# Opening of a two-layer trunk kernel: separate signals for constants, parameters and tokens, and the two parts of the first modulation computed in another order

## The chip, the core and the metric

The program runs on one core of a Trainium2 chip. The metric is the device time of one execution in microseconds (us). A core has TensorE (PE in the profile, its weight loads PEld), VectorE (DVE), ScalarE (ACT), GpSimd (POOL) and SyncE (SP), which here issues nearly all DMA transfers. They run side by side and wait for each other through semaphores. A DMA adds 16 to its semaphore when it has landed.

## What is computed

The reference runs two layers of a trunk. What stands at its very start is the part that matters here:

```python
mod = jax.nn.silu(c) @ w_mod[i] + b_mod[i]
mod_c = jax.nn.silu(c_ctx) @ w_mod[i] + b_mod[i]
sh1, sc1, g1, sh2, sc2, g2 = jnp.split(mod[:, None, :], 6, axis=-1)
h = _modulate(_rmsnorm(x, norm1_g[i]), sh1, sc1)       # h * (1 + scale) + shift
hc = _modulate(_rmsnorm(xc, norm1_g[i]), sh1c, sc1c)
y, yc = _mixer(h, hc, ...)                             # begins with h @ w_in
```

with `_rmsnorm(x, g) = x * rsqrt(mean(x * x) + EPS) * g`. There are 256 latent and 256 context tokens of 1024 channels. After the mixer (a state-space branch and a retention branch) each layer has a product-key expert stage, which takes most of the time.

## The kernel before

Tokens lie transposed in `xT`: 128 partitions, 8 channel blocks (`KD`), 512 tokens. Weights come in units of 128 x 2048 floats (1 MB) into `ring`, which has four slots. SP loads unit u into slot u mod 4 once `used[slot]` says that the unit four places earlier has been read. The modulation matrix of a layer is 24 such units, four (`MOD_W`) for each of the six parts: units 0 to 3 give the shift `sh1`, units 4 to 7 the scale `sc1`.

The work is ordered by hand: every engine has its own block, which walks the same list of stages. The opening is the stage `mod`, then `norm1`, then `front`.

- **SP** (L634 to L646): constants `cst`, parameters `par`, tokens `xT` (2 MB), all on the one semaphore `const_in`, then w_mod units 0 to 7 through the ring, then the first unit of `w_front` and the later units, in the order in which their slots come round.
- **PE**: waits for all three (`const_in` at 48). `norm_mean` multiplies the squares of the tokens with a matrix of 1/1024 (8 matmuls of 512 columns, which the trace shows as 16). `mod_row_of` makes one 256-wide piece of a modulation row from one unit, reading the condition `cond0`, and frees the slot. `mod_columns` turns the finished row `mrow0` into columns, one small matmul for each block of 128 channels. Then come the front products of `norm1`'s result with w_front unit 0: the high part of the weights times the high part of the tokens (`wX`, `hiP`), the low part of the weights (`elo`), then the low part of the tokens (`loP`), then two more modulation units.
- **ACT**: silu of the condition, `cond0`, the squares `hT` (L1480), the state-space parameters (L1554 to L1561), the square root of the mean (`stddev`, L1486, into `rs1`), copies of each row piece from PSUM (L1535), the high part of w_front unit 0 (`front_high`, L1514), and then `shifted` (L1498): token plus shift, into `hiP`.
- **DVE**: the state-space parameters, the reciprocal of `rs1` (`inverted`, L1986), `mod_tables` (L2005 to L2012: bias added, and the gain from the scale), `normed` (L1997: `xT` times gain times `rs1`, 16 halves of 256 tokens), the low part of w_front unit 0 (`front_low`, L2020), and `loP` (L2086), which reads both `xT` and `hiP`.

## Time and profile before

| | us |
|---|---|
| median of 3 runs | 2993.99 |
| lowest and highest | 2991.23, 2996.83 |
| span of the profiled execution | 2986.2 |

| engine | busy us | share of the span |
|---|---|---|
| PE | 2762.6 | 93% |
| DVE | 2404.3 | 81% |
| ACT | 1409.5 | 47% |
| POOL | 405.5 | 14% |

The shares are means over the whole program, so they say little of its first 60 us, in which all that the change touches happens. For that stretch one reads the chain of work that ended last and the timeline. The span runs from the first to the last instruction; the device time has some 8 us more around it.

### The profile page before, as it was taken

Reading aid. Unit: us, or ns where it says so; the run is one execution under the profiler, and the core shown is the slowest. Engines: PE = TensorE matmul, PEld = TensorE weight load, DVE = VectorE, ACT = ScalarE, POOL = GpSimd, SP = SyncE. Lnnn points to the kernel's source line nnn. Section 1 sums busy time; section 2 is a strip of 40 time slices with the busy share of each in tenths; the row PEclk is TensorE's granted clock in tenths of the full one; section 3 lists DMA queues with packets and bytes.
Section 4 is the critical chain, followed back from the end, with each engine's and each line's share of the span. In section 5 each row is a group of like instructions: output and inputs, shape, how many; then the busy total and the mean of one; then the engine's idle time right before and its main releaser. Section 6 shows DMA issues by size and latency. Waiting matters only on the chain.

```text
span 2986.2 us, 52044 instructions
## 1 busy us (share of the span) xinstructions
PE 2762.6 (93%) x18077; PEld 2395.3 (80%) x18077; DVE 2404.3 (81%) x4652; ACT 1409.5 (47%) x2264; POOL 405.5 (14%) x408
## 2 busy tenths in 40 slices
PE   6999999777899999999999998989966999999998
PEld 5878877547788888888888886877855888888887
DVE  5487555998987888878888887787589888898887
ACT  5343432227744444444444444324426666666664
POOL 0000000005422211212212210000005101010110
PEclk9999999879999999999999999999987999999999
DMA  6522222644489898998888883323430688888885
GB/s 247 210 91 86 99 99 107 246 158 159 155 308 320 306 333 297 330 324 305 290 301 291 292 299 129 116 97 103 161 136 29 230 321 310 320 312 318 314 322 209
DMA packets 168663, 677.80 MB, mean 227 GB/s; under 512 B 16464, under 2 KB 50416, under 8 KB 125296
## 3 DMA queue, kind: packets, MB, share of 16 engines
q1 hardware_dynamic: 134816, 432.09, 40.3%
q0 software_dynamic: 33744, 244.37, 22.8%
q8 instruction: 61, 1.00, 0.1%
q14 instruction: 42, 0.34, 0.0%
HBM read 658.63 MB, written 17.69 MB: 226 GB/s over the span
## 4 chain that ended last, share of the span: by engine, by line
PE 80%; DVE 12%; DMA 3%; ACT 2%; issue 1%; SPq 0%; POOL 0%; ACTq 0%; DVEq 0%
PE ps L889 80%; DVE hot L2537 2%; DMA ring<-in_w_mod 1%; DVE hot L2532 1%; DVE hot L2535 1%; DVE loP L2086 1%; DMA gate_scratch<-spill 1%; DVE gst L2238 0%; DMA xT<-x_scratch 0%; DVE rs L1986 0%; DMA xT<-in_x_t 0%; PE ps L1026 0%; DMA mcst<-in_mixer_consts 0%; DVE elo L2032 0%; DVE hx L2249 0%
## 5 line engine op out<-in xcount | busy, mean ns | idle before, releaser
L889 PE MATMUL ps<-h2a,ehi 128*128 128x352 f32 x2048 | 492.6, 323 | 1.4 <-DVE elo L2547 1.4
L815 POOL DMA_INDIRECT gbuf<-in_expert_rows,gidx x192 | 236.1, 1230 | 1438.6 <-DVE yg L2592 1328.3
L1946 ACT ACTIVATE ehi<-ring 128x1024 fp32r<-128x1024 f32 x256 | 271.3, 1060 | 288.5 <-PE ps L889 288.1
L889 PEld LDWEIGHTS ps<-h2a,ehi 128*128 128x128 f32 x2048 | 359.9, 188 | 16.5 <-DVE elo L2547 1.9
L2604 DVE TENSOR_TENSOR elo<-ring,ehi 128x1024 fp32r<-128x1024 f32 x256 | 313.0, 1223 | 69.2 <-ACT ehi L1946 67.2
L889 PE MATMUL ps<-h2b,ehi 128*128 128x192 f32 x2048 | 348.2, 273 | 1.8 <-DVE elo L2547 1.8
L889 PEld LDWEIGHTS ps<-h2b,ehi 128*128 128x128 f32 x2048 | 321.3, 192 | 13.3 <-DVE elo L2547 2.1
L889 PE MATMUL ps<-h2a,elo 128*128 128x352 f32 x1024 | 328.7, 321 | 0.0
L2547 DVE TENSOR_TENSOR elo<-ring,ehi 128x1024 fp32r<-128x1024 f32 x256 | 311.9, 1219 | 14.0 <-ACT ehi L1911 14.0
L889 PE MATMUL ps<-h2b,elo 128*128 128x192 f32 x1024 | 281.8, 275 | 0.0
L1911 ACT ACTIVATE ehi<-ring 128x1024 fp32r<-128x1024 f32 x256 | 268.9, 1051 | 12.0 <-DMA ring<-in_experts 11.9
L2592 DVE SCALAR_TENSOR_TENSOR yg<-gbuf,gw,yg 128x1024 f32<-128x1024 f32 x192 | 245.8, 1280 | 25.9 <-ACT gw L1933 25.9
L889 PE MATMUL ps<-ehi,whA 128*128 128x512 f32 (+1 forms) x768 | 241.5, 395 | 2.3 <-DVE wlA L2628 2.3
L889 PE MATMUL ps<-ehi,wB 128*128 128x512 f32 x768 | 241.1, 395 | 0.0
L889 PE MATMUL ps<-ehi,wlA 128*128 128x512 f32 (+1 forms) x768 | 240.9, 394 | 0.0
L889 PE MATMUL ps<-elo,whA 128*128 128x512 f32 (+1 forms) x768 | 239.8, 393 | 0.0
L2582 DVE SCALAR_TENSOR_TENSOR gbuf<-gbuf,h2n 128x1024 f32<-128x1024 f32 x192 | 234.0, 1219 | 0.1
L889 PEld LDWEIGHTS ps<-h2b,elo 128*128 128x128 f32 x1024 | 197.2, 193 | 0.0
L889 PEld LDWEIGHTS ps<-h2a,elo 128*128 128x128 f32 x1024 | 192.5, 188 | 0.0
L889 PE MATMUL ps<-hot 128*128 128x128 f32 x1088 | 148.5, 291 | 38.4 <-ACT hot L1898 32.1
L889 PEld LDWEIGHTS ps<-hot 128*128 128x128 f32 x1088 | 136.5, 199 | 50.8 <-issue 39.6
L889 PEld LDWEIGHTS ps<-elo,whA 128*128 128x128 f32 (+1 forms) x768 | 137.7, 179 | 41.1
(444 smaller groups left out, 5368.5 us busy)
## 6 DMA issues: line engine op xcount, KB each, us to landing
ring<-in_experts SPq DMA_DIRECT2D x512, 512.0 KB, 6.1
ring<-in_w_mod SPq DMA_DIRECT2D x48, 1024.0 KB, 5.9
ring<-in_w_side SPq DMA_DIRECT2D x24, 1024.0 KB, 5.0
ring<-in_w_front SPq DMA_DIRECT2D x12, 1024.0 KB, 6.4
ring<-in_w_merge SPq DMA_DIRECT2D x16, 768.0 KB, 4.3
ring<-in_w_q SPq DMA_DIRECT2D x12, 1024.0 KB, 7.4
gate_scratch<-spill SPq DMA_DIRECT2D x44, 256.0 KB, 2.0
gateA<-gate_scratch SPq DMA_DIRECT2D x4, 2816.0 KB, 18.2
```

Source lines behind the costliest of these rows:

```text
L815: pool.indirect_dma_start(gbuf[:, k % 2, :], None, a[f"expert_rows{l}"], bass.IndirectOffsetOnAxis(gidx[:, at:at + 1], 0)).then_inc(gather ...
L889: return pe.matmul(out, w, x, start=start, stop=stop, **k)
L1911: act.activation(ehi[:, k % 2, :], ring[:, (u + k) % RING, 0:DM], ACT.Copy).then_inc(uhi_ready, 1)
L1946: act.activation(ehi[:, 2 + k % 2, :], ring[:, (u + k) % RING, DM:2 * DM], ACT.Copy).then_inc(vhi_ready, 1)
L2086: last = v.scalar_tensor_tensor(by_four(loP[:, k, :], s_), by_four_of(scaled(l, k, s_)), modT[:, l, 0, k, side:side + 1], by_four(hiP[:, k ...
L2532: v.tensor_tensor(hot[:, g, 1, 0:2, :], row.unsqueeze(1).to_broadcast([P, 2, P]), idxT[:, 1, 4 * n:4 * n + 2].unsqueeze(2).to_broadcast([P ...
L2535: v.tensor_scalar(hot[:, g, 1, 2, :], row, idxT[:, 1, k:k + 1], idxT[:, 2, k:k + 1], ALU.is_equal, ALU.mult)
L2537: v.tensor_tensor(hot[:, g, 0, :, :], row.unsqueeze(1).to_broadcast([P, 4, P]), idxT[:, 0, 4 * n:4 * n + 4].unsqueeze(2).to_broadcast([P, ...
L2547: v.tensor_tensor(elo[:, r, 0:DM], ring[:, r, 0:DM], ehi[:, k % 2, :].bitcast(F32), ALU.subtract).then_inc(ulo_ready, 1)
L2582: v.scalar_tensor_tensor(rows, rows, 1.0, h2n[:, :], ALU.mult, ALU.mult, accum_out=ga[:, at]).then_inc(dot_ready, 1)
L2592: v.scalar_tensor_tensor(yg[:, :], gbuf[:, n % 2, DM:2 * DM], gw[:, at], yg[:, :], ALU.mult, ALU.add).then_inc(acc_done, 1)
L2604: v.tensor_tensor(elo[:, r, DM:2 * DM], ring[:, r, DM:2 * DM], ehi[:, 2 + b, :].bitcast(F32), ALU.subtract).then_inc(vlo_ready, 1)
```

## The change

Constants, parameters and tokens get semaphores of their own (`par_in`, `cst_in`, and `x_in[0]`, `x_in[1]` for the two halves of the channels). SP loads the parameters, the constants, the four units of the scale, the two halves of the tokens and then the four units of the shift. PE makes the scale's rows and columns, then the mean, then the shift's rows and columns (in PSUM bank 5). ACT moves the squares behind the state-space work and the scale's copies; it waits for the shift's table ahead of `shifted`. DVE makes the scale's table ahead of the reciprocal, and the shift's table inside `normed`, after three of the eight blocks. Two two-turn loops (on PE and ACT) and one on SP are written out.

```diff
-            sp.dma_start(cst[:, :], a["consts"]).then_inc(const_in, 16)
-            sp.dma_start(par[:, :], a["params"]).then_inc(const_in, 16)
-            sp.dma_start(xT[:, :, :], a["x_t"]).then_inc(const_in, 16)
+            sp.dma_start(par[:, :], a["params"]).then_inc(par_in, 16)
+            sp.dma_start(cst[:, :], a["consts"]).then_inc(cst_in, 16)
...
-                    stream(u, a["w_mod"][0, 0:EARLY], EARLY)
+                    for k in range(MOD_W):
+                        load(u + k, a["w_mod"][0, MOD_W + k])
+                    for n in range(2):
+                        part = slice(n * KD // 2, (n + 1) * KD // 2)
+                        sp.dma_start(xT[:, part, :], a["x_t"][:, part, :]).then_inc(x_in[n], 16)
+                    for k in range(MOD_W):
+                        load(u + MOD_W + k, a["w_mod"][0, k])
...
-            pe.wait_ge(const_in, 48)
+            pe.wait_ge(cst_in, 16)
...
+                    def part_columns(s, rows, bank):
+
+                        count(pe, mod_row, rows)
+                        for c in range(s * KD, (s + 1) * KD):
+                            last = mm(ps[:, bank, 2 * c:2 * c + 2], mrow0[:, c * P:c * P + P], cst[:, C_SEL:C_SEL + 2], True, True)
+                        last.then_inc(mod_col, 1)
+
+                    pe.wait_ge(cond_ready, 1)
+                    for k in range(MOD_W):
+                        mod_row_of(u + k, k, k, cond0)
+                    part_columns(1, MOD_W, 4)
                     norm_mean(("norm1", 0, 0), hT, TL)
-                    pe.wait_ge(cond_ready, 1)
-                    mod_rows(u, 0, 0, EARLY, 0, cond0)
-                    mod_columns(0, 0, 2, mrow0, 4)
+                    for k in range(MOD_W):
+                        mod_row_of(u + MOD_W + k, MOD_W + k, k, cond0)
+                    part_columns(0, 2 * MOD_W, 5)
...
-            act.wait_ge(const_in, 48)
+            act.wait_ge(cst_in, 16)
+            act.wait_ge(par_in, 16)
...
+                    elif k % (KD // 2) == 0:
+                        act.wait_ge(x_in[k // (KD // 2)], 16)
...
+                if st == ("norm1", 0, 0):
+                    act.wait_ge(mod_done, 2)
...
-                    squares(("norm1", 0, 0), hT, 0, TL)
...
+                    rows_of(1, 0)
+                    squares(("norm1", 0, 0), hT, 0, TL)
                     stddev(("norm1", 0, 0), rs1, TL)
-                    mod_rows(u, mrow0, 0, EARLY, 0)
+                    rows_of(0, MOD_W)
...
-            dve.wait_ge(const_in, 48)
+            dve.wait_ge(cst_in, 16)
+            dve.wait_ge(par_in, 16)
...
-                if st != ("norm1", 0, 0):
-                    inverted(st, rs, w)
+                inverted(st, rs, w)
                 for k in range(KD):
+                    if st == ("norm1", 0, 0) and k == 3:
+                        mod_tables(0, 0, 1, ps[:, 5, 0:2 * KD], 2)
...
-                    inverted(("norm1", 0, 0), rs1, TL)
-                    mod_tables(0, 0, 2, ps[:, 4, 0:4 * KD], 1)
+                    mod_tables(0, 1, 2, ps[:, 4, 2 * KD:4 * KD], 1)
```

`rows_of(part, first)` is ACT's copy of four row pieces. The rest of the diff counts `mod_col` and `mod_done` one higher in the later stages, since there is one more table.

On PE, from the start of the program, before. `ring,cond` is a modulation unit (8 matmuls), `cst,mrow` the columns, `hT,cst` the mean, and the last three rows are the products of w_front unit 0:

```order
1 L889 MATMUL ps<-hT,cst 128x512 x8
...
5 L889 MATMUL ps<-ring,cond 32x256 x8
6 L585 REGISTER_ALU
7 L889 MATMUL ps<-ring,cond 32x256 x8
8 L585 REGISTER_ALU
9 L889 MATMUL ps<-ring,cond 32x256 x8
10 L585 REGISTER_ALU
11 L889 MATMUL ps<-ring,cond 32x256 x8
12 L913 REGISTER_ALU
13 L913 COMPARE_AND_BRANCH
14 L889 MATMUL ps<-cst,mrow 128x2 x16
15 L889 MATMUL ps<-wX,hiP 128x256 x32
```

And now, in the same place:

```order
1 L895 MATMUL ps<-ring,cond 32x256 x32
2 L895 MATMUL ps<-cst,mrow 128x2 x8
3 L895 MATMUL ps<-hT,cst 128x512 x8
4 L895 MATMUL ps<-ring,cond 32x256 x32
5 L895 MATMUL ps<-cst,mrow 128x2 x8
6 L895 MATMUL ps<-wX,hiP 128x256 x32
7 L895 MATMUL ps<-elo,hiP 128x256 x32
8 L895 MATMUL ps<-wX,loP 128x256 x32
```

The mean has moved from the first place to behind four units and half of the columns, and the other four units stand behind it (before, rows 5 to 11 were a loop of two turns).

On ACT, from the start of the parameters' work, before:

```order
3 L1528 ACTIVATE cond<-par 128x8x2
4 L1480 ACTIVATE hT<-xT 128x512 x8
5 L1554 ACT_TABLE_LOAD
6 L1554 ACTIVATE lg<-par 128x16
7 L1555 ACTIVATE lg<-lg 128x16
8 L1557 ACTIVATE s5w<-par 128x64
9 L1559 ACTIVATE s5w<-s5p 128x64
10 L1560 ACT_TABLE_LOAD
11 L1560 ACTIVATE s5w<-s5w 128x64
12 L1561 ACTIVATE s5w<-s5w,cst 128x64
13 L1486 ACT_TABLE_LOAD
14 L1486 ACTIVATE rs<-ps,cst 128x512
```

And now, from the last of the state-space work:

```order
11 L1582 ACTIVATE s5w<-s5w,cst 128x64
12 L1589 ACTIVATE mrow<-ps 128x256 x4
13 L1500 ACTIVATE hT<-xT 128x512 x8
14 L1506 ACT_TABLE_LOAD
15 L1506 ACTIVATE rs<-ps,cst 128x512
16 L1589 ACTIVATE mrow<-ps 128x256 x4
17 L1536 ACTIVATE wX<-ring 128x2048
18 L1520 ACTIVATE hiP<-xT,modT 128x64x4 x16
```

The squares stand behind the scale's four copies, and the conversion of w_front's first unit stands, as before, behind the last copies and ahead of `hiP`.

On DVE, now, from the last of the state-space work to `loP`:

```order
31 L2108 TENSOR_TENSOR s5p<-s5w 128x64
32 L2037 TENSOR_TENSOR modT<-ps,par 128x16
33 L2043 TENSOR_SCALAR gain<-modT 128x16
34 L2044 TENSOR_TENSOR gain<-gain,par 128x16
35 L2017 RECIPROCAL rs<-rs 128x512
36 L2029 SCALAR_TENSOR_TENSOR xT<-xT,gain,rs 128x256 x6
37 L2037 TENSOR_TENSOR modT<-ps,par 128x16
38 L2029 SCALAR_TENSOR_TENSOR xT<-xT,gain,rs 128x256 x10
39 L2052 TENSOR_TENSOR elo<-ring,wX 128x2048
40 L2117 SCALAR_TENSOR_TENSOR loP<-xT,modT,hiP 128x64x4 x16
```

Before, the reciprocal stood ahead of one table for both parts, and the 16 halves of `xT` in one row behind it.

## Rows read from the trace of the kernel before

**Rows 1.** Chain that ended last, 0 to 110 us: start us, us, what.

```profile
1.65 9.99 DMA xT<-in_x_t
...
13.39 12.81 PE ps L889 x80
...
26.21 9.80 DMA ring<-in_w_mod
...
36.13 1.11 PE ps L889 x16
...
37.79 3.75 PE ps L889 x32
...
42.28 6.43 DVE xT L1997 x16
48.70 2.20 DVE elo L2020
50.91 9.58 DVE loP L2086 x16
60.49 0.04 issue
60.53 49.64 PE ps L889 x449
```

**Rows 2.** Timeline: start us, us, engine, line, operation, count [idle before <-releaser].

```profile
11.66 0.21 ACT L1551 ACTIVATE par<-par 128x16 f32<-128x16 f32 x1 [9.63 <-DMA xT<-in_x_t]
12.63 4.25 ACT L1480 ACTIVATE hT<-xT 128x512 f32<-128x512 f32 x8
13.39 9.17 PE L889 MATMUL ps<-hT,cst 128*128 128x512 f32 x16 [13.39 <-ACT hT L1480]
```

**Rows 3.** DMA totals of 0 to 12 us, then of 20 to 40 us.

```profile
DMA packets 574, 3.74 MB, mean 312 GB/s; under 512 B 60, under 2 KB 188, under 8 KB 316
...
ring<-in_w_mod SPq DMA_DIRECT2D x6, 1024.0 KB, 4.9
ring<-in_w_front SPq DMA_DIRECT2D x2, 1024.0 KB, 8.7
```

**Rows 4.** Timeline: modulation units on PE, ACT's copy, the columns.

```profile
28.68 1.07 PE L889 MATMUL ps<-ring,cond 128*32 128x256 f32 x16 [2.53 <-DMA ring<-in_w_mod]
31.16 1.93 PE L889 MATMUL ps<-ring,cond 128*32 128x256 f32 x16 [1.41 <-DMA ring<-in_w_mod]
37.36 0.38 ACT L1535 ACTIVATE mrow<-ps 128x256 f32 x1 [1.64 <-PE ps L889]
37.79 3.73 PE L889 MATMUL ps<-cst,mrow 128*128 128x2 f32 x32 [0.59 <-ACT mrow L1535]
```

**Rows 5.** Weight loads of the mean on PE, two slow ones and two fast ones.

```profile
15.23 0.33 PEld L889 LDWEIGHTS ps<-hT,cst 128*128 128x128 f32 x1 [0.52 <-issue]
16.08 0.33 PEld L889 LDWEIGHTS ps<-hT,cst 128*128 128x128 f32 x1 [0.52 <-ACT hT L1480]
...
18.11 0.19 PEld L889 LDWEIGHTS ps<-hT,cst 128*128 128x128 f32 x1 [0.24 <-issue]
18.54 0.19 PEld L889 LDWEIGHTS ps<-hT,cst 128*128 128x128 f32 x1 [0.24 <-issue]
```

**Rows 6.** Stretches: window, us, busy (x instructions) of each engine, PEclk, DMA share, GB/s.

```profile
26.20:36.10 9.90, 4.54 (x48) 1.68 (x48) 6.04 (x12) 3.07 (x9) 0.00 (x0) 0.83 1.01 427
42.30:50.80 8.50, 5.67 (x25) 4.90 (x26) 8.50 (x17) 7.61 (x15) 0.00 (x0) 0.65 0.34 138
50.80:61.20 10.40, 9.30 (x73) 8.56 (x72) 10.40 (x18) 8.87 (x19) 0.00 (x0) 1.00 0.00 0
61.20:75.00 13.80, 13.80 (x137) 12.60 (x140) 13.70 (x25) 5.12 (x7) 0.00 (x0) 1.00 0.60 230
```

**Rows 7.** Timeline: from the deviation to the end of the first front unit.

```profile
26.36 0.69 ACT L1486 ACTIVATE rs<-ps,cst 128x512 f32<-128x512 f32 x1
29.26 3.35 DVE L1986 RECIPROCAL rs<-rs 128x512 f32<-128x512 f32 x1
38.52 1.91 ACT L1514 ACTIVATE wX<-ring 128x2048 fp32r<-128x2048 f32 x1 [0.78 <-DMA ring<-in_w_front]
43.19 8.40 ACT L1498 ACTIVATE hiP<-xT,modT 128x256 fp32r<-128x256 f32 x16 [2.77 <-DVE xT L1997]
52.22 3.93 PE L889 MATMUL ps<-elo,hiP 128*128 128x256 f32 x32
55.98 3.02 PE L889 MATMUL ps<-wX,loP 128*128 128x256 f32 x24
61.20 1.93 PE L889 MATMUL ps<-ring,cond 128*32 128x256 f32 x32
```

More of the change, by code:

```diff
@@ L473, in build_program @@
         ps = ctx.enter_context(nc.psum_tensor("ps", [P, 8, 512], F32))
-        const_in = sem("const_in")
+        cst_in, par_in = sem("cst_in"), sem("par_in")
+        x_in = [sem(f"x_in{k}") for k in range(2)]
         unit_in = [sem(f"unit_in{s}") for s in range(RING)]
@@ L1562, in _, with rows_of @@
                                    bias=cst[:, C_HPI:C_HPI + 1]).then_inc(s5_trig, 1)
+                    def rows_of(part, first):
+                        for k in range(MOD_W):
+                            unit_used(act, u + first + k)
+                            at = DM * part + 256 * k
+                            act.activation(mrow0[:, at:at + 256], ps[:, k, 0:256], ACT.Copy).then_inc(mod_row, 1)
+                    rows_of(1, 0)
+                    squares(("norm1", 0, 0), hT, 0, TL)
                     stddev(("norm1", 0, 0), rs1, TL)
-                    mod_rows(u, mrow0, 0, EARLY, 0)
+                    rows_of(0, MOD_W)
                 elif kind == "norm1":
@@ L1613, in _ @@
                     if l == 0:
-                        act.wait_ge(mod_col, 2)
+                        act.wait_ge(mod_col, 3)
                         act.activation(mcol[:, :], ps[:, 6, 2 * 2 * KD:2 * 5 * KD], ACT.Copy).then_inc(mod_out, 1)
@@ L2210, in skips @@
                     def skips():
-                        dve.wait_ge(mod_col, 2)
+                        dve.wait_ge(mod_col, 3)
                         v.tensor_tensor(dsk[:, :, :], cst[:, C_DIAG:C_DIAG + 16].unsqueeze(1).to_broadcast([P, 16, 16]),
@@ L2363, in _ @@
                         dve.wait_ge(mod_out, 1)
-                        mod_tables(0, 2, 5, mcol[:, :], 2)
+                        mod_tables(0, 2, 5, mcol[:, :], 3)
                 elif kind == "merge":
@@ L2475, in _ @@
                     if next_route(st):
-                        mod_tables(0, 5, 6, ps[:, 3, 10 * KD:12 * KD], 3)
-                        mod_tables(1, 0, 2, ps[:, 2, 0:4 * KD], 4)
+                        mod_tables(0, 5, 6, ps[:, 3, 10 * KD:12 * KD], 4)
+                        mod_tables(1, 0, 2, ps[:, 2, 0:4 * KD], 5)
                         normed(next_route(st), rs2, 256, h2T, 0, lambda k, s: gain[:, l, 1, k, s:s + 1], h_scaled)
@@ L2517, in _ @@
                         s0, s1 = MOD_PARTS[st]
-                        mod_tables(1, s0, s1, ps[:, 2, 2 * s0 * KD:2 * s1 * KD], 4 + half)
+                        mod_tables(1, s0, s1, ps[:, 2, 2 * s0 * KD:2 * s1 * KD], 5 + half)
                 elif kind == "gates":
```

## The prediction, made before the changed kernel ran

> **What bounds the kernel now.** I read the chain that ended last first [rows 1]. In the opening it goes through the 2 MB of tokens until 11.64 us, then PE until 26.2 us (the mean, and the first four modulation units), then 9.80 us of waiting for the other four units, one unit and the columns on PE, and three pieces of DVE work: `xT`, `elo`, `loP`. From 60.53 us the chain is PE for 50 us without a gap. So what the opening takes until the first front unit is done goes straight into the end, and nothing behind it waits for something that has its own clock: the weights behind it are loaded when PE frees their slots. While PE works on the first front unit DMA moves nothing in 50.8 to 61.2 us [rows 6], all four slots being full, so later loads move together with PE.
>
> The timeline then shows two wasted times. All engines wait 9.6 us or more for the tokens [rows 2], though the silu of the condition needs only 188 KB of parameters. And DMA is idle for a while because the second four units wait for slots that PE frees only after the mean. From there it runs at 427 GB/s, a unit each 2.45 us (1.05 MB over 427 GB/s) [rows 6].
>
> **Part 1: what lands when.** By 12 us 3.74 MB had been moved [rows 3]. Constants, parameters and tokens are 0.58 + 2.10 = 2.68 MB, yet the tokens landed only at 11.64 us, 2.1 us later than the 9.5 us at which 2.68 MB had been moved (3.74 less 2.5 us of 0.427 MB each): the 16 engines are not abreast, and a transfer lands with its slowest one. I carry the 2.1 us along. The first four units now come at once behind the constants: 0.58 + 4.19 = 4.77 MB, that is 12 + 1.03/0.427 + 2.1 = 16.5 us for the last of them (and 9.2, 11.6, 14.1 us for the others). The token halves follow at 19.0 and 21.4 us, the shift's units at 23.9, 26.3, 28.8 and 31.2 us, since their slots are freed by 18.5 us, before the backlog ends. Before, the last of these units was read at 36.13 us [rows 1], so 5 us of the transfers' time are won. The tokens, in return, land nearly 10 us later.
>
> **Part 2: scale and mean on PE.** The last scale unit costs PE 1.07 us at 2.4 GHz or 1.93 us at 1.2 GHz [rows 4]; I take 1.5, so 18.0 us. ACT's copy is 0.38 us [rows 4]. The scale's columns are half of the 3.73 us [rows 4], 1.87 us: PE is ready for the mean at 20.3 us. The squares are 0.53 us a block (4.25/8) [rows 2]; the first four are done by 21.2 us and the last four, behind the second half, by 23.6 us, ahead of PE's pace. The mean took 9.1 us before, the first five matmuls 0.85 us apart and the other eleven 0.43 us [rows 2, 5]. All slow it would be 13.6 us, all fast 6.9 us. Here I choose the 9.1 us again, because a few short bursts with waits between them have fallen to the half clock before (PEclk 0.83 in 26.2 to 36.1 us, with one unit at 1.93 us) [rows 4, 6]. So the mean ends at 29.4 us, where it ended at 22.5 before. This is the price of the change: 6.9 us.
>
> **Part 3: who is last for `hiP`.** ACT can start `shifted` (43.19 us before [rows 7]) when four things are there.
> - Deviation and reciprocal: 29.4 + 0.7 + 0.1 + 3.35 = 33.5 us [rows 7], and one block of `xT` 0.8 us (6.43/8 [rows 1]): 34.3 us.
> - The shift's table: four units of 1.07 us, of which the last landed at 31.2 us, end at 33.7 us; copy 0.4, columns 1.87, table 0.2: 36.2 us. DVE reaches its place in `normed` (three blocks) at 35.9 us, so it stops 0.3 us for it. The wait has the other five blocks of `xT` queued behind it on DVE, and `loP` behind those.
> - The high part of w_front unit 0. Its slot is freed by the first shift unit, after the mean: 29.4 + 1.07 = 30.5 us. A load into an emptied queue landed in 4.9 us; one that had units ahead of it in 8.7 us [rows 3]. The last shift unit lands at 31.2 us and leaves room at 33.7, so 4.9 us decides: 35.5 us. The conversion is 1.91 us [rows 7]: 37.5 us with the signals. Before, this lay hidden behind the columns; now it is last.
> - ACT itself, free of its copies by 34.1 us.
>
> For that load the Trainium skill has a price too: "DMA: Bandwidth & Descriptors", section Bandwidth, gives 6.15 us for 1 MB alone, measured on GpSimd's kind of queue. By it the sum would gain 1.2 us less. The row of this kernel's own queue has 4.9 us, and the row decides.
>
> So `hiP` starts at 37.5 instead of 43.19 us: 5.7 us earlier.
>
> **Part 4: the first front unit.** Before, PE ended `hiP` at 52.4 us, then 3.93 us for `elo`, overlapping a little, and began `loP` at 55.98; 32 matmuls at 3.02/24 would be 4.03 us and end at 60.0 us, but DVE's `loP` held it and the next piece began at 61.20 us [rows 7]. Now DVE is earlier by more: 33.5 + 6.43 + 0.4 for `xT`, 2.2 for `elo`, 9.6 for `loP` [rows 1] is 52.1 us, and PE's last block 0.8 later 52.9 us; PE by itself needs 60.0 - 5.7 = 54.3 us. PE is last, and another 1.2 us are won: 6.9 us in all at the place where the 50 us of PE begin. The loops written out, the reordered constants and the one more table are under 0.3 us together and lie beside waits; I cost them at nothing.
>
> **The sum.** 6.9 us off 2986.2 gives a span of 2979.3 us. The profiled span is 7.8 us below the median of 2993.99, for what lies around it and for scatter, and I take the gain off the median: **2987.1 us**.
>
> **Rivals.**
> - *The clock is at its upper level all the time.* Last scale unit read by 17.6, columns done by 19.9, mean 6.9 us: 26.8 us. Then `hiP` no longer hangs on the mean but on the queue: w_front unit 0 lands one unit behind the last shift unit, 33.7 us, converted 35.7 us; 7.5 + 1.2 = 8.7 us gained, 2985.3. For it: the units come every 2.45 us and one of them took 1.07 us after a gap [rows 4].
> - *The clock stays at its lower level through the mean.* Last scale unit read by 18.4 us, copy, columns at twice their time 3.7 us: 22.5 us; mean 13.6 us: 36.1 us; shift unit 1.93, load 4.9, conversion 2.0: `hiP` at 45.0 us, 1.8 later than before. With the 1.2 us of part 4 it comes to a loss of 0.6 us: 2994.6, no change. Half of this (a mean of some 11.4 us) still gains 3 to 4 us. For it: units of this kind pulled PEclk to 0.83, and before `hiP` it fell so that 42.3 to 50.8 us show 0.65, behind the columns [rows 6]; the columns now stand right ahead of the mean. Against it: the mean went from slow to fast after its fifth matmul although PE had done nothing before it [rows 5]. The Trainium skill speaks for this rival: "TensorE: Matmul & The Clock Gate", section HAM oscillation, describes matmuls in short bursts with waits for DMA between them as falling back to the low level again and again. The trace agrees in the stretch of 26.2 to 36.1 us.
> - *Slower: the low clock carries into the front products.* PE ran 42.3 to 50.8 us at 0.65 without cost, since it waited for ACT there; `elo`, `loP`, the next units and front unit 1 (52 to 75 us) ran at 1.00 and are PE's alone [rows 6, 7]. Should they fall to the half clock, each 1 us of them costs 1 us more; 7 us of them take the gain away, and from 13 us on it is slower by what I can tell. All of 54 to 68 us at half would give 14 - 6.9 = 7 us more than now, 3001. Against it: PE was without a gap for all that time, and the clock rose in the same place before.
> - *The opening is shorter but the end is not*, because a later stage waits for something else. Nothing in the chain shows it; it would be 2994.
>
> **How the numbers follow.** Forecast with its neighbours (5 to 8 us) 0.50, upper clock 0.20 (with what could be won beyond it), lower clock through all or half of the mean 0.19, shorter opening without effect 0.06, slower 0.05. A measurement of this kernel tells about 0.2%, 6 us, from no change (the three runs lie within 5.6 us). The forecast lies hardly beyond that bound, so 0.34 of its 0.50 count as faster; with the upper clock that is 0.54. Same is 0.16 + 0.19 + 0.06 = 0.41, slower 0.05. The range holds the forecast, the upper clock and half of the lower clock, and 1.5 us of scatter at the lower end: 2983 to 2993.
>
> **What would show it.** Right: silu by 5 us; the last token half's squares after 21 us; the mean from about 20 to 29 us, with half-clock matmuls at its start; ACT idle until w_front lands at about 35.5 us, then `hiP` at 37.5; the first front unit done at 54.3 us with PE, not DVE, as the last; and every later stage 7 us earlier. Wrong: a mean that ends after 31 us (clock) or begins after 22 us (landing times of part 1, which rest on bytes and one lag); `hiP` released by the shift's table or by DVE and not by w_front; or a front stage with PEclk below 1.00.

## The result, and the profile of the changed kernel

| kernel | median us | lowest to highest | ratio to the kernel before, 95% interval |
|---|---|---|---|
| before | 2993.97 (4 runs) | 2991.23 to 2996.83 | |
| changed | 2978.28 (4 runs) | 2976.33 to 2980.86 | 0.9948 [0.9936, 0.9961] |

The change is faster by 15.7 us (12 to 19 by the interval). Forecast were 6.9 us and a range of 2983 to 2993: the sign was right, the size was less than half of what came, and the time lies below the range.

The profiled execution of the changed kernel has a span of 2979.0 us and took 2980.86, so 1.9 us lie around the span. Against the span of before, 2986.2, this is only 7.2 us. That the two pairs differ so much (7.2 us between the profiled executions, 15.7 between the medians) is the question of this study. In the first comparison below one execution of the changed kernel took 8814 us and one of the kernel before 3524 us, at mean granted clocks of 0.30 and 0.74, and the ratios are taken without these two.

First the opening. The chain that ended last in the changed kernel, 0 to 110 us (start us, us, what), beside [rows 1]:

```profile
3.08 14.02 DMA ring<-in_w_mod
...
33.75 4.93 DMA ring<-in_w_front
...
38.72 1.79 issue
40.52 8.48 ACT hiP L1520 x16
...
59.32 9.24 DMA ring<-in_w_front
...
68.58 1.93 ACT wX L1536
...
70.53 2.31 DVE elo L2052
...
73.19 13.45 PE ps L895 x128
```

The tokens' transfer, the 9.8 us for the second four units and `xT` on DVE have left the chain. In their place stand the scale's units, then PE, then the load of w_front unit 0 in 4.93 us and its conversion on ACT (an interval called issue here, 38.70 to 40.52), as part 3 had it. Behind 59 us the chain has changed too: where it was PE alone, it now goes through the loads of later w_front units, their conversion and `elo`. PE has no gap between 61 and 115 us in the kernel before, and 0.84 us of gaps (0.55 and 0.29 us, both for `elo`) in the same stretch of the changed kernel. The timeline shows the same steps with their sizes; beside [rows 2, 4, 7]:

```profile
4.57 0.22 ACT L1573 ACTIVATE par<-par 128x16 f32<-128x16 f32 x1
...
9.88 1.93 PE L895 MATMUL ps<-ring,cond 128*32 128x256 f32 x16 [9.88 <-DMA ring<-in_w_mod]
...
17.14 1.93 PE L895 MATMUL ps<-ring,cond 128*32 128x256 f32 x16 [0.55 <-DMA ring<-in_w_mod]
...
19.58 3.58 PE L895 MATMUL ps<-cst,mrow 128*128 128x2 f32 x16 [0.50 <-ACT mrow L1589]
...
22.09 2.19 ACT L1500 ACTIVATE hT<-xT 128x512 f32<-128x512 f32 x4 [0.30 <-DMA xT<-in_x_t]
...
23.01 9.67 PE L895 MATMUL ps<-hT,cst 128*128 128x512 f32 x16
...
38.70 1.91 ACT L1536 ACTIVATE wX<-ring 128x2048 fp32r<-128x2048 f32 x1 [1.97 <-DMA ring<-in_w_front]
...
57.32 1.93 PE L895 MATMUL ps<-ring,cond 128*32 128x256 f32 x32
```

The silu has moved from 11.66 to 4.57 us. The last scale unit is read from 17.14 us (16.5 forecast), the columns take 3.58 us, the time at 1.2 GHz, and the mean ends at 32.6 us. The first front unit ends at 57.32 instead of 61.20 us: 3.9 us in this pair, where 6.9 were forecast.

So in the one pair of traces the opening gives less than forecast, and the medians give more. Two theories were put against each other. **A**: all of it is the opening, and single executions scatter. **B**: the change also does something to stages far behind the opening.

### The profile page after: what moved, and what is told of

Read it like the earlier page. It is cut to its first block, busy times and chain, and to the rows that moved or that the text cites. A ratio compares the mean times of both kernels' runs of the same rounds, so it can differ in the third digit from the quotient of the medians.

```text
span 2979.0 us, 52023 instructions
## 1 busy us (share of the span) xinstructions
PE 2768.1 (93%) x18077; PEld 2398.4 (81%) x18077; DVE 2404.6 (81%) x4653; ACT 1410.3 (47%) x2264; POOL 405.0 (14%) x408
## 4 chain that ended last, share of the span: by engine, by line
PE 78%; DVE 15%; DMA 3%; ACT 2%; issue 1%; SPq 1%; POOL 0%; DVEq 0%; ACTq 0%
PE ps L895 77%; DVE hot L2568 2%; DVE hot L2563 1%; DVE hot L2566 1%; DMA ring<-in_w_mod 1%; DMA ring<-in_w_front 1%; DVE topi L2452 1%; DVE topi L2460 1%; DVE sc L2454 0%; DVE top L2457 0%; DVE top L2449 0%; DMA gate_scratch<-spill 0%; DVE elo L2052 0%; DVE rs L2017 0%; PE ps L1043 0%
## 5 line engine op out<-in xcount | busy, mean ns | idle before, releaser
L895 PEld LDWEIGHTS ps<-h2a,ehi 128*128 128x128 f32 x2048 | 361.0, 189 | 16.5 <-DVE elo L2578 1.9
## 6 DMA issues: line engine op xcount, KB each, us to landing
gateA<-gate_scratch SPq DMA_DIRECT2D x4, 2816.0 KB, 17.9
```

The lines of the kernel that those rows point to most:

```text
L895: return pe.matmul(out, w, x, start=start, stop=stop, **k)
```

## The experiments

### The same kernel again, and a delay in its opening

> The changed kernel once more, beside the kernel before on the same chip. In the profiles the first front unit ends 3.9 us earlier (57.3 against 61.2 us), the spans differ by 7.2 us and the medians by 15.7 us. Theory A (the opening passes on its 4 us, the rest is scatter between executions and chips): here the medians differ by 3 to 8 us. Theory B (the change moves something in the later stages too): 12 to 17 us again.

```diff
                 if st == ("norm1", 0, 0):
                     act.wait_ge(mod_done, 2)
+                    for k in range(2 * KD):
+                        own.link(act.activation(hT[:, k % KD, :], cst[:, 0:512], ACT.Copy))
```

> The changed kernel with 16 copies of 128x512 on ScalarE ahead of the shift's additions, some 9 to 11 us in the chain of the opening (a square of that size took 0.61 us, each now also waits for the one before). What the opening costs is passed on one to one (A): it ends 9 to 11 us later than the changed kernel, 2 to 6 us behind the kernel before. If later stages take it up (B): less than half of it arrives at the end.

The changed kernel took 2979.0 us, before 2992.9: ratio 0.9950 [0.9937, 0.9964], 13.8 us by the medians. It was run once more in a later comparison:

> The changed kernel again, for a closer interval beside the kernels with one loop written out and as the base of the next version. Three comparisons so far gave 13 to 16 us. Expected 12 to 16 us below the kernel before, of which some 4.5 us belong to the loops (e1_loops) and the rest to the new order.

2977.6 us against 2992.8, 0.9950 [0.9937, 0.9963]. So 14 to 16 us it is, on three occasions, and A's 3 to 8 us is out.

The delayed kernel took 2989.7 us, 10.7 us more than the changed kernel beside it. The copies took 10.5 us:

```profile
39.80 10.53 ACT L1514 ACTIVATE hT<-cst 128x512 f32<-128x512 f32 x16
50.36 8.43 ACT L1522 ACTIVATE hiP<-xT,modT 128x256 fp32r<-128x256 f32 x16
```

What is spent in the opening arrives at the end one to one. This part of the prediction, that all stages behind move rigidly, holds. But its expected place, 2 to 6 us behind the kernel before, was missed: with 10.5 us added to the chain the kernel was still 0.9986 [0.9977, 0.9995] of before.

### How long the old opening is

> The kernel before, unchanged, as one of the kernels tried: what two runs of one kernel differ by, and a second look at its opening. In the first profile the 32 columns matmuls took 3.7 us and the first front unit ended at 61.2 us; in the kernel with written-out loops the columns took 7.0 us at PEclk 0.50 and it ended at 65.7 us. If that is the clock's phase and not the loops (A), this profile shows the columns anywhere between, and the timing no difference above 1 us. If the loops do it (B), the columns are 3.7 us again.

The kernel before against itself: 2992.4 against 2993.9, 0.9995 [0.9986, 1.0004]. Its second profile is almost the first one, 60.90 us to the end of the first front unit and columns of 3.7 us. That is what was expected if the loops make the difference. But other kernels in the old order, each traced once, speak against it: with TensorE's loop in place the columns took 4.65 us (e3_sploop), 6.17 (e2_signals) and 6.32 (e4_actloop), and 7.0 us in the two with that loop written out. This is the timeline of the kernel with only its loops written out (below), and then the stretch of 36 to 44 us (PEclk is the third number from the end) of the kernel before and of that one:

```profile
39.68 6.99 PE L890 MATMUL ps<-cst,mrow 128*128 128x2 f32 x32 [0.50 <-ACT mrow L1568]
```

```profile
36.00:44.00 8.00, 4.80 (x48) 4.08 (x48) 2.26 (x8) 3.10 (x4) 0.00 (x0) 0.84 1.01 418
```

```profile
36.00:44.00 8.00, 6.95 (x45) 4.92 (x37) 0.00 (x0) 2.68 (x3) 0.00 (x0) 0.50 1.01 418
```

At 0.50, 1.2 GHz, the columns cost 3.3 us more, and in the old order they stand on the chain with all 32 passes: behind them come the tables, `xT` and everything else. In the changed kernel the clock at the columns does differ from execution to execution: the first 16 passes took 3.58, 2.58 and 1.95 us in its three traces. For the kernel before itself this isn't shown by a trace, since both of its traces have 3.7 us for the 32. Time at which the first front unit had ended, one profiled execution each:

| old order | us | new order | us |
|---|---|---|---|
| before | 61.20 | changed | 57.32 |
| e2_null | 60.90 | e1_after | 54.75 |
| e3_sploop | 61.92 | e3_after | 53.60 |
| e4_actloop | 64.14 | e4_order | 54.98 |
| e1_loops | 66.34 | | |
| e3_peloop | 67.26 | | |
| mean | 63.6 | mean | 55.2 |

The difference of the means is 8.5 us; the pair before and changed alone has 3.9. The first trace of the changed kernel has the longest opening of the new order. The two traces of the kernel before have the shortest of the old order, and both come from short executions: some 2988 and 2987.7 us, where its medians are 2992 to 2995. Its executions also scatter more than those of the changed kernel (2985.7 to 2999.0 us, 23 of them, against 2976.6 to 2979.8, six, in one comparison). So its median execution is likely to have a longer opening than 61 us. No such execution was traced, and the mean of 63.6 us is one of six traces of five kernels, not of this kernel.

### What the half clock costs in either order

```diff
+                        for _w in range(1 if k else 3):
+                            mm(ps[:, 6, :], cst[:, C_ID:C_ID + P], cst[:, 0:512], True, True)
                         mod_row_of(u + k, k, k, cond0)
```

> The changed kernel with six matmuls more that nobody reads (128x512, three ahead of the first scale unit and one ahead of each of the next three), in PE time that was idle. In the profile of the changed kernel the scale units took 1.93 us, the columns 3.6 and the mean 9.7 us, with its first matmuls 0.85 us apart. If the price of the new order is the half clock (A): units 1.07, columns 1.9, mean 6.9 us, the mean's end 5 to 6 us earlier (26.5 to 27.5 us), the conversion of the first front unit 4 to 5 us earlier, and the end 4 to 5 us earlier than the changed kernel. If the clock is not what it costs: the mean ends where it did, and there is no gain.

2977.1 us, 0.9949 [0.9936, 0.9962], against 0.9950 for the changed kernel beside it: no difference that can be told. The filling matmuls did what they should up to the fourth unit (units of 1.07 us), and then the clock fell all the same:

```profile
16.78 1.07 PE L895 MATMUL ps<-ring,cond 128*32 128x256 f32 x16 [0.37 <-DMA ring<-in_w_mod]
...
18.35 2.70 PE L895 MATMUL ps<-cst,mrow 128*128 128x2 f32 x16 [0.50 <-ACT mrow L1591]
...
20.91 9.71 PE L895 MATMUL ps<-hT,cst 128*128 128x512 f32 x16
```

The lower level comes while PE does the columns, which load 128-wide weights and multiply two columns each, and the mean behind them starts slow. The experiment thus didn't remove what it was meant to remove, and leaves open what the mean's slow start costs at the end. The mean ended at 30.6 us, 26.5 to 27.5 expected.

In the old order the same was tried, two such matmuls ahead of the fifth unit and one ahead of each of the last three, loops written out:

> The kernel before with loops written out, and six matmuls of 128x512 that nobody reads, in PE time that was idle: two ahead of the first DMA-paced shift or scale unit and one ahead of each of the next three. A: the columns take 3.7 us, the units 1.07 us, the first front unit ends at 60 to 61.5 us, and the time is 3 to 5 us below the same kernel without them (2988.5), that is 2983.5 to 2985.5. If the half clock in the opening costs nothing at the end: 2988.5 again.

2985.4 us, 0.9978 [0.9969, 0.9987]; the same kernel without them had 0.9985 [0.9976, 0.9993] in another comparison. The units took 1.07 us, the columns 4.62, the first front unit ended at 61.24 us instead of 66.34. Not all of that is the filling: the mean had begun at 11.18 us and not at 13.48, since the tokens landed earlier in this execution, and the last unit was read 1.9 us earlier. The 2 to 3 us go the expected way, but the intervals overlap.

### One part of the change alone

Only the signals apart and the tokens in halves, everything in the old order:

```diff
-            sp.dma_start(xT[:, :, :], a["x_t"]).then_inc(const_in, 16)
+            for n in range(2):
+                part = slice(n * KD // 2, (n + 1) * KD // 2)
+                sp.dma_start(xT[:, part, :], a["x_t"][:, part, :]).then_inc(x_in[n], 16)
...
```

> The kernel before with only the signals apart and the tokens in two halves, all in the old order (loops kept). The silu starts at 4 to 5 us and not at 11.7; the squares start when the first half lands, at 7 to 9.5 us. The second half lands at 11.7 us and the mean ends 0.5 to 3 us earlier; the last shift or scale unit is still bound by its slot, which the mean frees: it lands 0.5 to 3 us earlier, and so does all the rest. A: 0.5 to 3 us faster than before. B, that the order of the modulation parts is what matters: no difference.

2991.4 us, 0.9991 [0.9982, 1.0000]. The last unit was read at 32 us and not at 36, but the columns behind it took 6.2 us, and the first front unit ended at 59.56 us. By the interval the signals alone are worth 0 to 5 us.

The written-out loops alone:

```diff
-                    mod_rows(u, 0, 0, EARLY, 0, cond0)
+                    for k in range(EARLY):
+                        mod_row_of(u + k, k, k % RING, cond0)
```

and likewise ACT's copies and SP's loads.

> The kernel before with nothing but its three two-turn loops of the opening (on SyncE, TensorE and ScalarE) written out, as the change also does. A: no difference above 1 us. B, if the place of the later instructions or the loops matter: a good part of the 15.7 us, at least 4.

2988.5 us, 0.9985 [0.9976, 0.9993]: 4.4 us faster, although its opening in the profile was 5 us longer than that of before. Theory A has no room for this. The prediction had put the loops at nothing. Comparing the traces between the same matmuls of the program, counted from the end, the 4 to 6 us lie in a few places far behind the opening. The plainest is at 1925 us. In the kernel before, a row of small matmuls that wait for nothing stops for 1.24 us:

```profile
1923.07 1.07 PE L889 MATMUL ps<-gk,xT 128*32 128x112 f32 x45
...
1924.07 0.50 PE L889 MATMUL ps<-gk,xT 128*32 128x112 f32 x8
1925.82 0.39 PE L889 MATMUL ps<-gk,xT 128*32 128x112 f32 x6 [1.24 <-issue]
1926.14 1.09 PE L1026 MATMUL ps<-cst,qk 128*128 128x128 f32 x8
```

DMA moves one piece of 0.02 MB on an instruction queue during that row; the queue's row for 1923 to 1927 us of the kernel before:

```profile
q8 instruction: 1, 0.02, 1.5%
```

This led to theory **C**: the change moves PE's later instructions in its stream, and with them the points at which PE waits for its next instructions.

The times of the pieces on that queue (q8, 16 KB each) bear on it. They follow TensorE's own count: between two of them it does 260 of its matmuls and weight loads on the mean (12 pieces around the stop), but 448 between the last two ahead of the stop. The first of these two came at 1894.4 us, 549 instructions ahead of the row's end, the second at 1923.57 us, just as a load of weights ran out that had kept DMA busy from 1920 us on. PE stopped at 1924.57 us and went on 1.3 us after the piece had moved (1.2 to 1.5 us in all five traces that have the stop). So PE ran dry some 540 instructions behind the last piece that came ahead of the load. In the thirteen traces without the stop that piece lies 334 to 463 instructions ahead of the row's end and not 549 to 559 as in the five; 540 instructions from it end behind the row, and the next piece comes before that, again as the load runs out. So the trace supports theory C for this stall. That the load holds the piece up is read from the times; no run takes the load away.

"Place" below means that instructions were added to or taken from TensorE's stream ahead of the row.

### Loops, order or place

> The kernel before with only TensorE's loop of the opening written out. In the three profiled kernels that have the loops, PE stands still for 1.2 to 1.7 us at 1925 us, in a row of matmuls that wait for nothing, and the mixer constants take 8.0 to 8.1 us to land at 116 us; in the six without, neither (6.6 to 6.9 us). If the place of PE's instructions makes the first (theory C: the loops matter by where the later instructions come to lie, each engine for its own): the stall at 1925 us is gone, the 8.0 us stay, 1.5 to 3 us faster than before. If it is the state of the chip: both stay.

> The kernel before with only SyncE's loop of the opening written out. Theory C: the mixer constants land in 6.7 us and not 8.0, the stall of PE at 1925 us stays, 1 to 2.5 us faster than before. Otherwise: 8.0 us and no gain.

> The kernel before with only ScalarE's loop of the opening written out. If the remaining 2 to 3 us of the written-out loops are ScalarE's: the stretch from the constants of the mixer to the first taps (31.0 us in the kernels with that loop, 28.7 to 29.7 without any loop) and the one at 764 to 811 us (44.6 to 47.1 against 43.5 to 44.5 us) get 1 to 2 us shorter each, PE's stall at 1925 us stays, and the time is 1.5 to 3.5 us below before. If they need all three loops gone: no difference.

| loop written out | us, before beside it | ratio | stall at 1925 us |
|---|---|---|---|
| TensorE's | 2990.8, 2992.8 | 0.9994 [0.9983, 1.0004] | gone |
| SyncE's | 2991.9, 2992.8 | 0.9996 [0.9985, 1.0007] | there |
| ScalarE's | 2992.6, 2992.9 | 0.9997 [0.9988, 1.0006] | there |

The stall goes with TensorE's loop alone. The mixer constants' landing (8.0 to 8.1 us at 116 us in the kernel before) did not follow SyncE's loop as expected: 8.2 us with it written out, 7.6 with TensorE's. None of the three is measurably faster alone, and with ScalarE's the two stretches that its expectation names didn't get shorter. With TensorE's the stall is gone, but the time from the end of the first front unit to the end of the span was 2926.5 us, against 2925.0 in the kernel before: the rest of that stretch had taken up what the stall gave back. Its opening (67.26 us) was long besides.

The new order with its loops back:

```diff
-                    for k in range(MOD_W):
-                        mod_row_of(u + MOD_W + k, MOD_W + k, k, cond0)
+                    mod_rows(u + MOD_W, 0, MOD_W, MOD_W, 0, cond0)
```

and likewise for the scale, for ACT's copies and for SP's last four loads.

> The changed kernel with its rows and loads in loops again, as the kernel before has them (now loops of one turn: two on TensorE, two on ScalarE, one on SyncE). If order and loops are two separate gains: 8 to 11 us faster than the kernel before, 4 to 6 us slower than the changed kernel (2977.6), and the first front unit ends at 54 to 58 us as in the changed kernel. If the loops are no cause: 14 us faster again.

2978.8 us, 0.9955 [0.9942, 0.9969]: 14.1 us faster than before, practically the changed kernel. Order and loops are not two gains that add. With loops and all, PE's instructions lie elsewhere than before, and the stall is gone. With the new order the loops don't matter; for e1_loops this makes another cause than the loops likely, but doesn't prove it.

Left to test is the place. Padding without touching a loop:

```diff
                     mod_columns(0, 0, 2, mrow0, 4)
+                    for c in range(32):
+                        mm(ps[:, 6, 0:2], mrow0[:, 0:P], cst[:, C_SEL:C_SEL + 2], True, True)
```

> The kernel before, loops kept, with 32 small matmuls that nobody reads behind the columns, in 3.0 us in which PE waits for hiP (they take 3.7 us at 2.4 GHz and up to 7 at 1.2, of which ScalarE's pace hides some). They move every later instruction of PE in its stream. If the place of the instructions makes the stall at 1925 us: it is gone, though the loop is there. If the loop as such does it: it stays. The time itself: within 3 us of before, since the padding costs up to some us in the opening.

The stall was gone with the loop in place. The padding itself cost 12 us: the first front unit ended at 73.35 us. The time was 2995.4, 2.5 us above before (1.0009 [1.0000, 1.0018]). Against the trace of before its span is 8.0 us longer, so 4.1 of the 12 us came back behind the opening, though in the delay experiment, which adds nothing on TensorE, nothing did. That the medians are only 2.5 us apart is one more sign that the traced opening of before, 61.2 us, is shorter than that of its median execution.

Cleaner, in the time in which PE waits for the tokens, on top of the kernel with only the signals apart:

```diff
+                    for c in range(8):
+                        mm(ps[:, 6, 0:2], cst[:, C_ID:C_ID + P], cst[:, C_SEL:C_SEL + 2], True, True)
                     norm_mean(("norm1", 0, 0), hT, TL)
```

> The kernel with the signals apart in the old order (e2_signals, 2991.4 us), with 24 small matmuls that nobody reads ahead of the mean, 4.8 to 10.5 us, where PE waits for the first half of the tokens until 8.9 us. If the place of TensorE's later instructions is what gives the later 4 to 6 us: the stall at 1925 us is gone, the time from the first front unit to the end is 2911 to 2918 us and not 2919 to 2924, and it is 3 to 7 us faster than e2_signals (2984 to 2988). If it is the loops or the new order: stall and 2991 us stay.

> The same with 8 small matmuls, a shift of a third of that. If the place matters by some grid, a small shift may leave the stall where it is or move it a little: either as e5_sig24, or the stall within the same row of matmuls at 1925 us but at another of them, and a time between 2985 and 2991 us.

With 8 of them: 2986.4 us against 2994.9, 0.9970 [0.9960, 0.9981]. This is a kernel in the old order, with its loops, to which nothing but useless instructions was added on top of the signals, and it is 8.5 us faster than before and, by the ratios (0.9991 and 0.9970, from two comparisons on different chips), some 6 us faster than with the signals alone. Its first front unit ended at 61.22 us, no earlier than before. The row of matmuls that stopped in before runs through:

```profile
1925.91 0.58 PE L892 MATMUL ps<-gk,xT 128*32 128x112 f32 x14
1926.42 1.09 PE L1031 MATMUL ps<-cst,qk 128*128 128x128 f32 x8
```

With 24 of them (48 passes, 10.4 us at the lower clock) the padding ran until 14.8 us and pushed the opening to 67.51 us. The stall was gone, the time 2992.0 us, 0.9989 [0.9979, 1.0000], not the 2984 to 2988 expected: the mean began 5.8 us later than with the signals alone, and the first front unit ended 8.0 us later. Behind the first front unit it needed 2922.5 us (2911 to 2918 expected), the kernel with 8 of them 2923.4 and the one without 2930.0.

The 18 traces were sorted by one thing, whether TensorE's instructions behind the opening lie where they did. The time from the end of the first front unit to the end of the span:

| | traces | us, mean | lowest to highest |
|---|---|---|---|
| place as before (before, e2_null, e2_signals, e3_sploop, e4_actloop) | 5 | 2926.6 | 2925.0 to 2930.0 |
| moved (the other 13) | 13 | 2922.0 | 2918.6 to 2926.5 |

In this time the two groups overlap, and the 13 differ among themselves by 7.8 us, which is more than the 4.6 us between the means and stays unexplained. The stall sorts without exception: it is in 5 of the 5 (1.24 to 1.73 us), each time ahead of the same matmul, the sixth from the end of its row, and in 0 of the 13. Between the same matmuls around it pass 25.8 to 26.5 us in the five and 24.3 in all thirteen: 1.9 us. Two other stretches differ in the same way without overlap: the first taps (115 to 146 us in before), 31.0 to 31.2 against 28.7 to 30.6 us, and the end of the gates' stage (764 to 811 us), 44.8 to 47.1 against 43.5 to 44.6. There the chain of before waits 4.03 us for its last spill of the gates (3.3 to 3.8 in the other four), and that of e3_after 1.98 us:

```profile
788.83 4.03 DMA gate_scratch<-spill
```

```profile
781.99 1.98 DMA gate_scratch<-spill
```

The three together are some 5 us. For the first taps and the gates it isn't shown that instructions arrive late; there only the sorting speaks. The first taps hold the landing of the mixer constants, which took 8.1 us in e5_sig8 as well, although its place is moved.

### A version meant to be better

```diff
                     for k in range(MOD_W):
+                        if k == 2:
+                            norm_mean(("norm1", 0, 0), hT, TL)
                         mod_row_of(u + k, k, k, cond0)
+                    mod_row_of(u + MOD_W, MOD_W, 0, cond0)
                     part_columns(1, MOD_W, 4)
-                    norm_mean(("norm1", 0, 0), hT, TL)
...
```

SP and ACT were ordered to match, and DVE makes the reciprocal ahead of the scale's table.

> A version meant to be better than the changed kernel: the tokens come behind two units of the scale and not behind four, PE makes the mean between them, the scale's columns behind the first unit of the shift, and DVE makes the reciprocal ahead of the scale's table. If the mean's end and the slot it frees are what binds the opening (A): the mean ends at 24 to 25 us and not at 30 to 32, the first front unit is loaded from 27 to 28 us, lands at 33 to 34 us, and hiP starts at 35.5 us and not at 38.1 to 40.5: 2 to 5 us faster than the changed kernel. If the 10 MB of transfers bind it, there is no gain.

2979.9 us, 0.9956 [0.9942, 0.9969], beside 2977.6 (0.9950 [0.9937, 0.9963]) for the changed kernel: not better. The mean ended at 21.9 us, even earlier than expected, but `hiP` began at 39.15 us:

```profile
30.56 1.93 PE L896 MATMUL ps<-ring,cond 128*32 128x256 f32 x16 [2.64 <-DMA ring<-in_w_mod]
32.89 1.93 PE L896 MATMUL ps<-ring,cond 128*32 128x256 f32 x16 [0.40 <-DMA ring<-in_w_mod]
35.33 3.58 PE L896 MATMUL ps<-cst,mrow 128*128 128x2 f32 x16 [0.50 <-ACT mrow L1592]
38.94 0.17 DVE L2042 TENSOR_TENSOR modT<-ps,par 128x16 f32<-128x16 f32 x1 [8.82 <-PE ps L896]
```

The last two shift units wait for slots that the scale's last two, now behind the tokens, free late. They and the columns are read at the half clock, and the shift's table comes last. The transfers bind, as the second theory had it, together with the clock. No kernel here beats the changed one by more than the measurement tells.

## Why the prediction was right and wrong, point by point

**What lands when: right.** Forecast were 9.2, 11.6, 14.1 and 16.5 us for the scale's units. PE began them at 9.88, 12.19, 14.66 and 17.14 us in the first profile and at 9.3, 11.6, 14.1 and 16.55 in e3_after. The 2.1 us by which a transfer lands behind its bytes carried over. The shift's last unit landed about 1 us later than the 31.2 us forecast (PE read it at 32.19 us in e3_after), without effect.

**The mean: right in its size, late in its place at first.** 20.3 to 29.4 us forecast; 23.0 to 32.6, 20.5 to 30.3 and 20.4 to 29.1 us in the three traces. The difference is the clock in the scale's units and columns. With 23.0 and 32.6 us the first trace passes two of the prediction's own signs of being wrong (a mean that begins after 22 or ends after 31 us); the other two traces don't.

**Who is last for `hiP`: right.** w_front unit 0, in 4.93 us (4.9 forecast), and its conversion. The 6.15 us that the Trainium skill has for 1 MB ("DMA: Bandwidth & Descriptors", section Bandwidth, on GpSimd's kind of queue) is more than this queue took. `hiP` began at 40.5, 38.1 and 36.9 us, forecast 37.5; the first front unit ended at 57.3, 54.8 and 53.6 us, forecast 54.3. PE, not DVE, was last there, and the 1.2 us of part 4 came: from `hiP`'s start to the end of that unit 18.0 us before, 16.7 to 16.8 in the three traces. It is close: in e3_after the shift's table was ready only 0.9 us ahead of the conversion's end, and the chain view goes through DVE's `xT` there and not through w_front.

**The base it was taken from: wrong, the step "so `hiP` starts at 37.5 instead of 43.19 us".** The new end was right within a microsecond of the mean of 55.2 us; the old one was 63.6 us on the mean of six traces in the old order and not 61.2, since its columns ran at 1.2 GHz for all or part of their time in four of the six. I had weighed the clock carefully on the side of the new kernel, where it isn't known, and taken it from one trace on the side of the old one. By these means the new order gains 8.5 us and not 6.9.

**The median and the span: wrong, the step "for what lies around it and for scatter".** The changed kernel's four runs show 1.9 us (1.8 in three) around the span. The first profiled execution of before thus took some 2988 us, 6 us below its median. That distance was the warning that it was an uncommonly good execution; I read it as a constant and subtracted from the median what I had reckoned from the trace.

**The loops and the rest "at nothing": wrong.** The PE chain at 60 to 110 us was right for the kernel before; in the changed one `elo` already holds PE for 0.84 us there. And PE's gap at 1925 us hangs on what stands ahead of it in its stream; the stretch behind the opening as a whole was 4.6 us shorter on average where that had changed, which is in none of my cases. Its direction was luck: nothing in the diff is for it.

Together: 8.5 + 4.6 = 13 us by the traces' means, and with 1.8 us around the spans 63.6 + 2926.6 + 1.8 = 2992.0 for the old kernel and 55.2 + 2922.0 + 1.8 = 2979.0 for the new one, against 2993 and 2978 to 2979 measured. These means are taken over different kernels, and how well they meet is in part luck. The two kernels' own traces give 61.1 + 2925.0 + 1.8 = 2987.8 us (two traces) and 55.2 + 2921.8 + 1.8 = 2978.8 us (three), 9 us apart: 5.8 us in the opening and 3.2 us behind it. The new kernel's sum meets its median; the old one's is 5 us short. The time behind the opening agreed within 0.5 us between traces of the same kernel, so those 5 us are most likely a longer opening in the executions of the old kernel that were not traced. That is an inference, and how the 14 to 16 us divide stays open by as much.

**The rivals.** The clock's rival with no gain did not come, though half its premise did: the columns ran at 1.2 GHz in the first trace (3.58 us, 2.58 and 1.95 in the other two), and so did the mean's first matmuls. It failed because the mean went fast again each time: it took 9.67, 9.84 and 8.81 us, never the 13.6 of that rival. The slower one, half clock in the front products, did not come: `elo` and `loP` took 3.93 and 4.00 us.

## What to carry to other kernels

One trace is one execution: before a gain is counted off it, look at how its own time stands to the median, and ask which terms on its chain ran at the clock's upper level by luck. An order that takes such terms off the chain gains in the bad executions too, not only in the one that was traced. And when a change adds or removes instructions on an engine, some us can come or go far behind it: compare the stretches between the same instructions, and try a few useless instructions more before crediting the idea: eight small matmuls went with some 6 us here, and 24, whose own time was larger, with nothing.

## What the runs showed of the hardware

- PE can stop in mid-row for 1.24 to 1.73 us without a wait that the profile shows, in a stretch where it takes in small matmuls quickly (45 in 1.07 us, each with its weight load). Five traces have the stop, always ahead of the same matmul, and go on 1.2 to 1.5 us after a piece of 16 KB on instruction queue 8 has moved, which had come late, behind a load of weights. The thirteen with instructions added or taken away ahead of it don't have it. "Runtime: NRT & Kernel Launch" of the Trainium skill, section Instruction fetch mechanics, says that instructions are refilled in blocks of 16 KiB and that this is mostly hidden. The size agrees with the row of 0.02 MB. That it is hidden doesn't hold in this place.
- Column matmuls (128-wide weights, two columns each) don't hold the clock up, although PE is busy with them. In e4_pad 96 passes without a gap took 20.64 us, the pace of the lower level from end to end:

```profile
39.57 20.64 PE L889 MATMUL ps<-cst,mrow 128*128 128x2 f32 x96 [0.59 <-ACT mrow L1537]
```

  In e1_warm PE had run units at 1.07 us until 17.9 us, and its columns took 2.70 us instead of 1.9. In the kernel before, all 32 passes still ran at the upper level.
- Those 32 passes took 3.73 us at the upper and 6.99 us at the lower level, so the weight loads slow down with the clock too.
